# Last down products of a feed-forward stage in two halves of four output chunks, with part of the next norm's work inside them

## The reference, cut to what matters

```
def rms_norm(x, g, eps=NORM_EPS):
    xf = x.astype(jnp.float32)
    y = xf * lax.rsqrt(jnp.mean(xf * xf, axis=-1, keepdims=True) + eps)
    return (y * g.astype(jnp.float32)).astype(x.dtype)

def swiglu(h, w_in, w_out):
    a, b = jnp.split(h @ w_in, 2, axis=-1)
    return (jax.nn.silu(a) * b) @ w_out

for i in range(DEPTH_2):
    h = adaln(x, norm_g[i, 0], shift[:, 0], scale[:, 0])
    x = x + MACARON_W * gate[:, 0, None] * swiglu(h, ffn_w_in_2[i, 0], ffn_w_out_2[i, 0])
    ...            # the mixer of this layer, with its own adaln
    h = adaln(x, norm_g[i, 2], shift[:, 2], scale[:, 2])
    x = x + MACARON_W * gate[:, 2, None] * swiglu(h, ffn_w_in_2[i, 1], ffn_w_out_2[i, 1])
```

## Time and the profile before

| | before |
|---|---|
| median of 3 runs | 3370.04 us (3366.2 to 3370.48) |
| profiled execution | 3369.03 us, span of its instructions 3367.2 us |
| PE busy | 3104.3 us, 92% |
| VectorE busy | 2325.2 us, 69% |
| ScalarE busy | 1590.2 us, 47% |
| GpSimd busy | 134.5 us, 4% |
| mean granted TensorE clock | 0.934 of full |

### The profile page before, as it was taken

The page is one execution under the profiler, slowest core; times in us unless marked ns, Lnnn a source line. Parts: engine busy times, 40 slices in busy tenths (PEclk is TensorE's granted clock), DMA queues, the critical chain, the costliest instruction groups (busy, mean ns, idle before and its releaser), DMA issues. The chain is left out here.

```text
span 3367.2 us, 63367 instructions
## 1 busy us (share of the span) xinstructions
PE 3104.3 (92%) x26673; PEld 2901.4 (86%) x26673; DVE 2325.2 (69%) x3472; ACT 1590.2 (47%) x2268; POOL 134.5 (4%) x152
## 2 busy tenths in 40 slices
PE   7679999889898899999988999999899999988899
PEld 6567777689887799999976999999699998977899
DVE  6568999767776467677578477775667677674544
ACT  4437777544552344444553344444544444442443
POOL 0010000000102000000000000000000001011000
PEclk8779999989999899999986999999899999998899
DMA  9347999757510267577430376774057577300441
GB/s 382 143 174 282 367 370 368 306 222 302 215 69 4 94 249 302 218 303 272 157 133 1 124 308 262 261 307 193 27 232 302 225 304 277 117 2 4 170 176 78
DMA packets 77527, 698.87 MB, mean 208 GB/s; under 512 B 8432, under 2 KB 12528, under 8 KB 55408
## 3 DMA queue, kind: packets, MB, share of 16 engines
q1 hardware_dynamic: 30928, 525.65, 39.8%
q10 hardware_dynamic: 42912, 157.31, 12.3%
q0 software_dynamic: 3456, 12.58, 1.0%
HBM read 691.31 MB, written 4.19 MB: 207 GB/s over the span
## 5 line engine op out<-in xcount | busy, mean ns | idle before, releaser
L1225 DVE TENSOR_TENSOR w_split<-ring,w_split 128x1024 fp32r<-128x1024 f32 x513 | 626.5, 1224 | 413.0 <-ACT w_split L1136 409.6
L1136 ACT ACTIVATE w_split<-ring 128x1024 fp32r<-128x1024 f32 x513 | 540.9, 1057 | 775.9 <-PE banks L1066 586.7
L1064 PE MATMUL banks<-u_split,w_split 128*128 128x256 f32 x2816 | 806.2, 286 | 15.9 <-DVE u_split L1285 13.2
L1065 PE MATMUL banks<-u_split,w_split 128*128 128x256 f32 x2816 | 804.0, 285 | 0.0
L1066 PE MATMUL banks<-u_split,w_split 128*128 128x256 f32 x2816 | 803.7, 285 | 0.0
L1064 PEld LDWEIGHTS banks<-u_split,w_split 128*128 128x128 f32 x2816 | 548.3, 195 | 20.8 <-DVE w_split L1225 10.9
L1065 PEld LDWEIGHTS banks<-u_split,w_split 128*128 128x128 f32 x2816 | 548.4, 195 | 0.4
L1066 PEld LDWEIGHTS banks<-u_split,w_split 128*128 128x128 f32 x2816 | 547.8, 195 | 0.0
L1064 PE MATMUL banks<-h_split,w_split 128*128 128x256 f32 x1408 | 398.8, 283 | 1.8 <-DVE w_split L1225 1.8
L1065 PE MATMUL banks<-h_split,w_split 128*128 128x256 f32 x1408 | 398.5, 283 | 0.0
L1066 PE MATMUL banks<-h_split,w_split 128*128 128x256 f32 x1408 | 398.5, 283 | 0.0
(11 more groups left out here) (489 smaller groups left out, 5037.9 us busy)
## 6 DMA issues: line engine op xcount, KB each, us to landing
ring<-stream SPq DMA_DIRECT2D x155, 3072.0 KB, 10.9
bufs<-ada ACTq DMA_DIRECT2D x296, 512.0 KB, 10.6
bufs<-ada POOLq DMA_DIRECT2D x23, 512.0 KB, 6.7
bufs<-ada SPq DMA_DIRECT2D x3, 2048.0 KB, 16.2
ring<-stream SPq DMA_DIRECT2D x2, 2688.0 KB, 9.6
bufs<-c_rows SPq DMA_DIRECT2D x9, 512.0 KB, 4.5
ring<-stream SPq DMA_DIRECT2D x1, 2704.0 KB, 13.7
ring<-stream SPq DMA_DIRECT2D x1, 2176.0 KB, 7.8
```

The costliest lines, as they stand in the source:

```text
L1064: pe.matmul(out, w(0), x(0), start=start, stop=False, skip_group_check=True)
L1065: pe.matmul(out, w(0), x(1), start=False, stop=False, skip_group_check=True)
L1136: nc.scalar.activation(w_split[:, slot, 0, :], piece(j, b), ACT.Copy).then_inc(high.sem, 1)
L1225: e = nc.vector.tensor_tensor(w_split[:, slot, 1, :], piece(j, b), w_split[:, slot, 0, :].bitcast(F32), ALU.subtract)
```

## The change

The last unit's down products get a function of their own. It waits for both low parts first, then does chunks 0 to 3 (f = 0, then f = 1), then chunks 4 to 7 (f = 0, then f = 1). Ahead of chunk 6 of the last part it puts the sums of the first pair of squares. `piece_used` for the f = 0 piece is raised when its second half is done. In the closing stages ScalarE does squares 0 to 3 ahead of its second weight piece of the next FFN. The remaining rows of the sums come in the order 2, 4, 5, 6, 7.

```
-    for c in (0, 4, 2, 5, 6, 7):
+    for c in rows:
...
-    last.then_inc(summed.sem, summed.count(1))
+    if c == KC - 1:
+        last.then_inc(summed.sem, summed.count(1))
...
+        self.rows = (0, 4, 2, 5, 6, 7)
...
+    def first_sums(self, pe):
+
+        if self.kind == "root":
+            paired_sums(self.core, pe, self.squares, self.bank, self.paired, self.squared, self.summed, (0,))
+            self.rows = (2, 4, 5, 6, 7)
...
-    def on_scalar(self, act):
+    def on_scalar(self, act, first=0):
         if self.kind == "root":
-            for c in range(KC):
+            for c in range(first, KC):
                 self.square(act, c)
...
+            def last_down_products():
+
+                pe.wait_ge(h_low.sem, h_low.at(n))
+                pe.wait_ge(low.sem, low.at(6 * n))
+                for first in (0, KC // 2):
+                    for f in range(2):
+                        for c in range(first, first + KC // 2):
+                            if f and c == KC - 2 and after:
+                                after.first_sums(pe)
+                            last = three(y[:, c, :], lambda part: w_split[:, f + 1, part, c * P:(c + 1) * P],
+                                         lambda part: h_split[:, (n - 1) % 2, part, f, :], start=False, stop=(f == 1))
+                            if f and c % 2:
+                                last.then_inc(y_done.sem, y_done.count(1))
+                        if first and f == 0:
+                            last.then_inc(piece_used.sem, 1)
...
-            down_products(n - 1, n, last_unit=True)
+            last_down_products()
...
                 for b in range(next_early):
                     act.wait_ge(piece_used.sem, piece_used.at(6 * n - 2 + b))
+                    if b and after:
+                        for c in range(KC // 2):
+                            after.square(act, c)
...
-                after.on_scalar(act)
+                after.on_scalar(act, KC // 2 if next_early else 0)
```

More of the change, by code:

```diff
@@ L747, in token_sums, with paired_sums @@
     last.then_inc(summed.sem, summed.count(1))
-def paired_sums(core, pe, squares, bank, paired, squared, summed):
+def paired_sums(core, pe, squares, bank, paired, squared, summed, rows):
     ones = core.const("ones")[:, 0:1]
-    for c in (0, 4, 2, 5, 6, 7):
+    for c in rows:
         if c < KC // 2:
@@ L836, in on_tensor @@
             inverse = core.event("inverse")
-            paired_sums(core, pe, self.squares, self.bank, self.paired, self.squared, self.summed)
+            paired_sums(core, pe, self.squares, self.bank, self.paired, self.squared, self.summed, self.rows)
             pe.wait_ge(inverse.sem, inverse.at(self.turn + 1))
@@ L1096, in first_up_products, with down_products @@
                     last.then_inc(piece_used.sem, 1)
-            def down_products(j, at, last_unit=False):
+            def down_products(j, at):
                 pe.wait_ge(h_low.sem, h_low.at(at))
                 for f in range(2):
-                    slot = (f + 1) % 3 if last_unit else (f + 2) % 3
-                    number = 6 * n - 2 + f if last_unit else down_piece(at, f)
-                    pe.wait_ge(low.sem, low.at(number + 1))
+                    slot = (f + 2) % 3
+                    pe.wait_ge(low.sem, low.at(down_piece(at, f) + 1))
                     for c in range(KC):
                         last = three(y[:, c, :], lambda part: w_split[:, slot, part, c * P:(c + 1) * P],
[L1107 to L1111, removed]
+                                     lambda part: h_split[:, j % 2, part, f, :],
+                                     start=False, stop=(f == 1))
+                    last.then_inc(piece_used.sem, 1)
[12 more added lines that the diff above has]
+                        if first and f == 0:
+                            last.then_inc(piece_used.sem, 1)
             first_up_products()
```

## The result

The changed kernel takes 3384.23 us in the median of 8 runs (3381.91 to 3389.4), the kernel before 3371.12 (8 runs with the first three, 3366.2 to 3377.82): 13.1 us slower. The ratio is 1.0042, with an interval from 1.0033 to 1.0051. The forecast's sum was +4.4 us, its likeliest outcome no measurable change, and its range ended at 3379. The direction of the sum was right, its size was a third of what came, and the time lies outside the range.

The account below looks back on a forecast made before the run. It took engine waits at the FFN stage ends, not TensorE's 92% busy share, as deciding: 4 x (+1.14) + 3 x 0 - 0.20 = +4.36 us, put at 3374.0 us, range 3368 to 3379.

Parts of the forecast that it names:

- The step that failed: Closing FFNs, ScalarE: squares 0 to 3 end at 4.49, the weight piece hides from 4.52 to 5.58, delaying only squares 4 to 7.
- Per end with a norm, from t0: 0.00: Seven FFN ends: counted from the last unit's start, the root comes at 9.07 us as before, so no cost.
- The rival of the sums inside the products: GpSimd's addition takes 1.71, TensorE waits 0.43 ahead of chunk 6, switches cost 0.24 each: +9.5 us, 3379; chance 0.12.
- the start wait: Four opening FFNs: TensorE waits for the second low part, so the last unit starts 1.14 us later in each.
- the zero cost for it in the closing and the last FFN: Closing and last FFNs: the second low part is done just in time, so waiting for both costs +0.
- the residuals in the new order: VectorE, from the last unit's start: residuals at 2.36, 2.76, 3.15, 3.55, 5.24, 5.63, 6.43, 6.82; the last 0.27 later.
- the last FFN's -0.20: Last FFN, without sums: residual 8 starts at 6.35 instead of 6.55 behind the last unit's start, 0.20 us gained.
- the table load as what ends last: Ends with a norm: ScalarE's table load behind the eighth square becomes the limit; the root waits for it until 9.07.
- the sums' saving that isn't used: Ends with a norm: sums inside the products save a real 0.26 us, unused because the table load is the limit.
- The price for a switch of TensorE to the sums and back: Inside the last unit's products: taken as 0; at the upper bound of 0.24 the seven ends cost 1.7 us.
- the clock: TensorE's granted clock halves behind stage ends; shifts deal its places anew, some +-0.9 us in single ends, near zero in sum.
- the rival of the clock falling inside the last unit: Opening FFNs: TensorE's longer pause drops its clock, 48 matmuls at 0.24 add 5.8 in four stages: +27, 3397; chance 0.03.

Follow-up runs that it names:

- e3: Changed kernel with ScalarE's squares 0 to 3 moved ahead of its wait for the used f = 0 piece in closing FFNs; 3378.64 us, 1.0029 to the kernel before.
- e1: Kernel before, with only the last unit's down products waiting for both low parts before they start; 3377.62 against 3371.95 us.
- e4: Changed kernel with each part waiting for its own low part and squares 0 to 3 ahead of ScalarE's wait; 3370.87 against 3371.95 us for the kernel before.
- e6: Changed kernel with both waits mended, plus a two-column root ahead of the squares to load the table early; 3371.53 against 3372.11 us for the kernel before.
- e5: Changed kernel with both waits mended and all 24 sum instructions behind the last product; 3373.83 against 3372.11 us for the kernel before, ratio 0.9999.

## Why the prediction was wrong

**The step that failed** is "In the closing stages ScalarE's second weight piece waits for the f = 0 piece, whose use ends with matmul 36 (4.20 + 0.32 = 4.52); squares 0 to 3 end at 4.49": it took the squares to be ahead of that wait. They are behind it: they start when the piece is used up, 4.52 behind t0, instead of 3.1 as in e3. The prediction's "Per end with a norm, from t0: 0.00" measured 1.13 in two of the three closing ends (root at 10.21 behind the mark against 9.08), and +3.9 over the three with what the clock did there. e3 moves the squares and gives back 5.6 us. The question asked of the wait, what stands behind it on its engine, was answered with "only squares 4 to 7" and had to be answered with all eight. The rival of the sums inside the products had the right symptom (TensorE idle ahead of chunk 6), but for a slow addition, which isn't it: the two additions took 1.41 here, against 1.51 before, but began late.

**Right:** the start wait. t0 moves as worked out and the opening roots come 1.1 later (4.4 of 4.56); e1 gets +5.7 from it alone. Right too are the zero cost for it in the closing and the last FFN (e1's closing roots don't come later), the residuals in the new order to 0.04 in the opening ends (in closing ones the first is 0.2 later, as VectorE was still at the next FFN's first piece, and the last two wait with TensorE), the last FFN's -0.20 (its last residual starts 6.44 behind the mark instead of 6.63), the table load as what ends last (e4, e6), and the sums' saving that isn't used. The price for a switch of TensorE to the sums and back, taken as 0, is 0 as near as the traces show: chunk 6's residual is 6.39 behind t0 in the changed kernel's opening ends, against 6.43 worked out. The drain behind a table load that the Trainium skill gives (ScalarE: Activation LUTs, "What ACT_TABLE_LOAD costs") is not in these traces: 0.01 to 0.02 lies between the load's end and the root.

**Mis-sized:** the clock, put at "near zero in sum". Behind the roots the changed kernel loses 2.65 (1.95 in the second profile), as the next stage begins over 1.7 behind the root in seven and five ends, against one and three before. In part it is the later root that meets the fall: in the opening ends of the kernel before's two profiles the clock fell 8.6 to 9.8 behind the mark, each time behind the start of the spread at 8.4; in the changed kernel's two it fell 8.0 to 11.1 behind the mark, and in six of eight ends ahead of the spread, which starts at 9.5. Four of these six falls came later than 8.4, where the spread would already have begun with the root in its old place. That the waits alone bring the loss about is not shown: e5, without either wait, had it in six ends, e4 in one.

**Not met:** the rival of the clock falling inside the last unit. TensorE's pause ahead of it was 1.6 us in four ends, and its matmuls behind it kept the pitch of 0.12.

## What to carry to other kernels

When work is put "ahead of" an instruction that waits, look whether it is ahead of the wait or only ahead of the instruction: on an engine that works in order, everything behind a wait is as late as what it waits for. When a loop over parts is turned inside out, give each part its own wait where it is first used: here 12 matmuls (1.44 us) were enough to hide the 1.14 us that one common wait at the top showed in full. And ask what ends last after the gain, before moving work: here neither early residuals nor early sums could bring the root forward, as a table load stood behind the last square.

## What the runs showed of the hardware beyond that

In the profiles of the kernel before, the granted clock falls to half 7.9 to 11.1 us behind the mark in each of the seven ends with a norm, and a microsecond more of work for TensorE ahead of the spread didn't keep it up: with three 128 x 512 products in front of the spread it fell at 1384.12 us, while they ended at 1384.16. An untouched stage of 137 us differed by 3.5 us between executions of one kernel, with the granted clock between 0.86 and 0.89; read from one profile of each kernel, the change would have cost 19.9 us, of which its seven ends account for 10.8.
